# 512-column passes over both parts of the moving tile, second feed-forward matrices by columns, smaller modulation loads, in a four-layer fp32 block program on one core

## The reference

```
x = x + concat(moba, mlstm, swa)(rms_norm(x, ln1) @ w_in) @ w_out
x = x + square(relu(rms_norm(x, ln2) @ w_up)) @ w_down            # 1024 -> 4096 -> 1024, two layers

mod = silu(c) @ w_ada + b_ada                                      # 6 vectors of 1024 for each layer
h = rmsnorm(x, norm1) * (1 + scale1) + shift1 ; p = h @ w_in       # 1024 -> 5632
x = x + gate1 * ((sigmoid(a) * (retention @ w_ret_o) + sigmoid(b) * (pool @ w_pool_o)) @ w_out)
h = rmsnorm(x, norm2) * (1 + scale2) + shift2
x = x + gate2 * ((silu(h @ w_gate) * (h @ w_value)) @ w_ffn_out)   # 1024 -> 2 x 2816 -> 1024, two layers
out = rmsnorm(x, final_norm)
```

## Time and profile before

| | |
|---|---|
| runs shown | 1609.57 us median of 3 (1604.56 to 1612.28) |
| profiled execution | 1605.11 us, of it the span 1603.3 us |
| granted TensorE clock, mean | 0.966 |
| TensorE passes (PE) | 1510.1 us, 11756 |
| weight loads (PEld) | 1444.4 us, 11756 |
| VectorE (DVE), ScalarE (ACT) | 1162.3 us, 790.5 us |
| DMA | 292.45 MB, mean 182 GB/s |
| first MLP; second | 202.9 to about 392; 575 to about 764 |
| feed-forwards of the second block | 985 to about 1178; 1403 to 1592 |

### The profile page before, as it was taken

The page is one execution under the profiler, slowest core; times in us unless marked ns, Lnnn a source line. Parts: engine busy times, 40 slices in busy tenths (PEclk is TensorE's granted clock), DMA queues, the critical chain, the costliest instruction groups (busy, mean ns, idle before and its releaser), DMA issues. The chain is left out here.

```text
span 1603.3 us, 28167 instructions
## 1 busy us (share of the span) xinstructions
PE 1510.1 (94%) x11756; PEld 1444.4 (90%) x11756; DVE 1162.3 (72%) x1907; ACT 790.5 (49%) x1208; POOL 10.5 (1%) x21
## 2 busy tenths in 40 slices
PE   5887999999987989999999999999999999999998
PEld 5875789999875679999999899999999999999997
DVE  4777768886778768877666787888876678775554
ACT  3544554444534554444646564444455666354443
POOL 2000000000000000000000000000000000000000
PEclk7997999999998899999999999999999999999999
DMA  8331278994532158986655556888666445556652
GB/s 242 103 107 64 68 225 287 303 287 138 153 106 92 51 191 275 300 278 208 172 157 149 154 158 211 268 289 272 224 173 180 146 145 157 157 174 185 187 186 75
DMA packets 382431, 292.45 MB, mean 182 GB/s; under 512 B 12749, under 2 KB 340689, under 8 KB 382049
## 3 DMA queue, kind: packets, MB, share of 16 engines
q1 hardware_dynamic: 380928, 287.01, 58.6%
q10 hardware_dynamic: 672, 1.97, 0.4%
q0 software_dynamic: 704, 1.66, 0.3%
HBM read 289.56 MB, written 1.05 MB: 181 GB/s over the span
## 5 line engine op out<-in xcount | busy, mean ns | idle before, releaser
L732 DVE TENSOR_TENSOR w_lo<-raw,w_hi 128x1024 fp32r<-128x1024 f32 x450 | 548.5, 1220 | 147.9 <-ACT w_hi L451 146.2
L451 ACT ACTIVATE w_hi<-raw 128x1024 fp32r<-128x1024 f32 x450 | 465.0, 1047 | 64.4 <-DMA raw<-in_w_out 29.6
L1331 PE MATMUL mx<-h_hi,w_hi 128*128 128x258 f32 (+1 forms) x1216 | 347.1, 285 | 8.0 <-DVE h_lo L753 7.3
L1331 PE MATMUL acc<-h_hi,w_hi 128*128 128x258 f32 (+1 forms) x1136 | 342.1, 301 | 10.5 <-DVE w_lo L732 5.3
L1333 PE MATMUL mx<-h_hi,w_lo 128*128 128x258 f32 (+1 forms) x1216 | 343.9, 283 | 0.0
L1332 PE MATMUL mx<-h_lo,w_hi 128*128 128x258 f32 (+1 forms) x1216 | 343.8, 283 | 0.0
L1333 PE MATMUL acc<-h_hi,w_lo 128*128 128x258 f32 (+1 forms) x1136 | 325.9, 287 | 0.0
L1332 PE MATMUL acc<-h_lo,w_hi 128*128 128x258 f32 (+1 forms) x1136 | 325.6, 287 | 0.0
L1339 PE MATMUL acc<-u_hi,w_hi 128*128 128x256 f32 x864 | 244.4, 283 | 1.4 <-DVE u_lo L1078 1.4
L1340 PE MATMUL acc<-u_lo,w_hi 128*128 128x256 f32 x864 | 242.1, 280 | 0.0
L1341 PE MATMUL acc<-u_hi,w_lo 128*128 128x256 f32 x864 | 242.0, 280 | 0.0
(11 more groups left out here) (257 smaller groups left out, 1854.3 us busy)
## 6 DMA issues: line engine op xcount, KB each, us to landing
raw<-in_w_in SPq DMA_DIRECT2D x132, 512.0 KB, 3.8
ada<-in_w_ada SPq DMA_DIRECT2D x48, 1024.0 KB, 6.6
raw<-in_w_ffn_in SPq DMA_DIRECT2D x88, 512.0 KB, 3.9
raw<-in_w_up SPq DMA_DIRECT2D x64, 512.0 KB, 6.5
raw<-in_w_down SPq DMA_DIRECT2D x64, 512.0 KB, 5.3
raw<-in_w_ffn_out SPq DMA_DIRECT2D x44, 512.0 KB, 3.4
raw<-in_w_out SPq DMA_DIRECT2D x32, 512.0 KB, 3.7
raw<-in_w_ret_o SPq DMA_DIRECT2D x16, 512.0 KB, 3.9
```

Source lines behind the costliest of these rows:

```text
L451: nc.scalar.activation(w_hi[:, n % NS], raw[:, n % NS], ACT.Copy).then_inc(hi_ready, 1)
L732: V.tensor_tensor(w_lo[:, n % NS], raw[:, n % NS], w_hi[:, n % NS].bitcast(F32), ALU.subtract).then_inc(lo_ready, 1)
L1331: mm(outp, wh, rhs_hi(k), start=k == 0, stop=False)
```

## The change

1. `h_hi`/`h_lo`, `y_hi`/`y_lo` and `u_hi`/`u_lo` become halves of one tensor with both parts of a tile side by side (`h2`, `y2`, `u2`). In the MLPs, the retention output, the second block's output and its feed-forward's output matrix, a tile takes one pass of `w_hi` over both parts (512 columns, a whole bank) and one pass of `w_lo` over the high part into the bank's second half (`both`, `slab_both`). Whoever reads the bank now adds its two halves: ScalarE copies one, VectorE adds the other, or VectorE adds both to x in turn. The projections, the pool slabs, `w_ffn_in` and the first block's output keep three passes.
2. `w_down` and `w_ffn_out` go by columns: first all 32 (44) slabs of the first matrix, with all of u kept on chip, then 32 (22) slabs, four (2.75) for each 128 output features, in three banks of `mx` in turn. A `w_ffn_out` slab that spans two chunks is loaded in two pieces. `row_slab`, `row_tail` and the orders `MLP` and `FFN` go. rstd is applied after the second matrix, squared (`rstd2`), in the MLP. Residual, norm and the next stage's operand follow tile by tile (`norm_hi_tile`, `low_tile`, `square_tile`) behind each chunk; the last transposes too.
3. Modulation weights come in 96 loads of 512 KB, spread over six stages: 48 products in each MLP, 16 in the first 16 projection slabs of each second-block layer, 48 and 16 in the feed-forwards. A group's sum stands on TensorE one position, its columns on VectorE two positions after its eighth product. TensorE waits for `ada_out` before `partners2(0)`.
4. In the pool slabs the rounding of `y_hi` moves from VectorE to ScalarE, behind it the low part, with a conversion between.

The core of the diff (other edits follow from these):

```diff
+ADA_UNITS = 4
+ADA_PLAN = {
+    ("A", 0): (0, 6, lambda q: 4 + q * 28 // 20 if q < 20 else 32 + q - 20),
+    ("A", 1): (6, 6, lambda q: 4 + q * 28 // 20 if q < 20 else 32 + q - 20),
+    ("P", 0): (12, 2, lambda q: 4 + q * 10 // 16),
+    ("F", 0): (14, 6, lambda q: 5 + q * 38 // 34 if q < 34 else 44 + (q - 34) * 18 // 14),
+    ("P", 1): (20, 2, lambda q: 4 + q * 10 // 16),
+    ("F", 1): (22, 2, lambda q: 6 + 2 * q),
+}
+def ada_loads(stage):
+    g0, n, at = ADA_PLAN[stage]
+    return [(NS + i if i < 3 else at(2 * i - 5) + 1 + NS, g0 * ADA_UNITS + i) for i in range(n * ADA_UNITS)]
+def ada_sums_at(stage, later):
+    g0, n, at = ADA_PLAN[stage]
+    return {at(8 * i + 7) + later: g0 + i for i in range(n)}
...
+                for d in range(32):
+                    n, s = divmod(d, 4)
+                    i = a_mlp[l] + MLP_UP + d
+                    load(i, raw[:, i % NS], wdown_v[:, l * 32 + 8 * s:l * 32 + 8 * s + 8, n * P:(n + 1) * P])
+                    ada_upto(pending, MLP_UP + d)
...
+                for j in range(MLP_UP // 2):
...
+                    hi_upto(at + AHEAD)
+                    act.wait_ge(slab_used, at + 2)
+                    nc.scalar.activation(sqt[:, 0], acc[:, b:b + 2, S:], ACT.Copy).then_inc(u_small, 1)
                     hi_upto(at + AHEAD + 1)
+                    act.wait_ge(u_pos, l * 16 + j + 1)
+                    nc.scalar.activation(t, t, ACT.Relu).then_inc(u_relu, 1)
+                    hi_upto(at + AHEAD + 2)
...
+                    lo_upto(at + AHEAD)
+                    dve.wait_ge(u_small, l * 16 + j + 1)
...
+                    V.tensor_tensor(ru[:, j % 2].rearrange("p (c t) -> p c t", c=2), acc[:, b:b + 2, 0:S], sqt[:, 0],
+                                    ALU.add).then_inc(u_pos, 1)
                     lo_upto(at + AHEAD + 1)
+                    if j:
+                        low(j - 1)
+                    ada_beside(2 * j)
+                    ada_beside(2 * j + 1)
+                    lo_upto(at + AHEAD + 2)
...
                     V.scalar_tensor_tensor(up[:, 0:S], up[:, 0:S], up[:, S:S + 1], gate[:, 0:S], ALU.add, ALU.mult).then_inc(g_prod, 1)
-                    while l == 0 and q < 64 and ada_step_b(q) == u:
-                        ada_product(128 + q)
-                        q += 1
-                    lo_upto(at + AHEAD + 2)
+                    ada_beside(2 * u)
+                    ada_beside(2 * u + 1)
+                    if u < 21:
+                        lo_upto(at + AHEAD + 2)
...
+            def both(bank, i, j, part, first, last):
+                mm(halves(bank), w_hi[:, i % NS, j], part, start=first, stop=False)
+                return mm(bank[:, S:], w_lo[:, i % NS, j], part[:, 0], start=False, stop=last)
...
+                sums = ada_sums_at(("P", l), 1)
+                for i in range(16):
+                    project(i)
+                    if i in sums:
+                        ada_sums(sums[i])
                 pe.wait_ge(bp_sh, e0 + 8)
+                pe.wait_ge(ada_out, (14, 22)[l])
                 partners2(0)
...
+                for s in range(FFN_IN):
...
+                    slab(f0 + s, h2, acc[:, s % 4, 0:W],
...
+                    ada_after(s)
```

More of the change, by code:

```diff
@@ L365, in load_ada @@
             def load_ada(e):
-                g, half = e // 2, e % 2
+                g, part = divmod(e, ADA_UNITS)
                 if e >= 3:
@@ L763, in boundary @@
                         norm_squares(v, b - 1)
[L764 removed]
+                    if b < 3:
                         norm_low(v, b, gain)
[L766 removed]
                 norm_squares(v, 3)
             def norm_squares(v, b):
[L770 removed]
+                dve.wait_ge(n_sq, N_SQ[v] + b + 1)
                 if b:
                     if b > 1:
[L773 removed]
+                        dve.wait_ge(n_acc, N_ACC[v] + b - 1)
                     V.tensor_tensor(ssq[:], ssq[:], sqt[:, b % 2], ALU.add).then_inc(n_acc, 1)
@@ L814, in ada_columns, with beside, work @@
                                 ALU.add).then_inc(ada_out, 1)
+            def beside(stage):
+                tiles, columns = ada_tiles(stage), ada_sums_at(stage, 2)
+                def work(p):
+                    for q in tiles.get(p, ()):
+                        ada_product(q)
+                    if p in columns:
+                        ada_columns(columns[p])
+                return work
             def norm_gain(l):
@@ L1100, in _ @@
+                low(MLP_UP // 2 - 1)
                 v = l * 2 + 2
@@ new lines, in _ @@
+                for d in range(32):
+                    n, s = divmod(d, 4)
+                    if n >= 3 and s == 0:
+                        pe.wait_ge(x_ready, 8 * (l * 2 + 2) + n - 2)
+                    slab_both(m0 + MLP_UP + d, lambda k: u2[:, 8 * s + k], mx[:, 1 + n % 3], first=s == 0, last=s == 3,
+                              before=(lambda k: pe.wait_ge(u_ready, l * 16 + 4 * s + k // 2 + 1)) if n == 0 else None,
+                              ).then_inc(slab_used, 1)
+                    ada_after(MLP_UP + d)
@@ new lines, in _ @@
+                    ada_after(s)
+                ends = 0
+                for d in range(22):
+                    i = f0 + FFN_IN + d
+                    pe.wait_ge(lo_ready, i + 1)
+                    for at, n, k0, count in ffo_runs(d):
+                        if n >= 3 and k0 == 0:
+                            pe.wait_ge(x_ready, 8 * (l * 2 + 6) + n - 2)
+                        for k in range(k0, k0 + count):
+                            if n == 0:
+                                pe.wait_ge(g_ready, l * 22 + k + 1)
+                            ins = both(mx[:, 1 + n % 3], i, at + k - k0, u2[:, k], k == 0, k == 21)
+                        if k == 21 and not FFO_WHOLE[n]:
+                            ins.then_inc(chunk_done, 1)
+                    ins.then_inc(slab_used, 1)
+                    ada_after(FFN_IN + d)
+                    if l == 1 and d >= 2 and d - 2 in FFO_END:
+                        to_tokens(FFO_END.index(d - 2))
```

589 lines of the change are left out of this document (308 added, 281 removed).

## The result

The changed kernel takes 1642.93 us (median of 4 runs, 1638.59 to 1649.5) against 1609.04 for the kernel before: a ratio of 1.0216, 95% interval 1.0174 to 1.0259. It is slower by 34 us, where I had forecast some 6 less, and it lies above my range (1579 to 1620).

A forecast was written before the change was run, and what follows sets the result against it. TensorE's number of passes times their pitch, plus its waits, was taken as the bound; gains of 46.6 us less costs of 40.7 gave net -5.9, 1605.1 to 1599.2, on the median 1604 us, range 1579 to 1620.

The forecast's parts named there:

- Passes: Converted tiles, MLPs and output stages: one 512- and one 256-column pass replace three of 256, gaining 34 us (bounds 0 and 36).
- a 512-column pass should cost 215: TensorE's converted tiles: a 512-column pass hides its weight load and takes 215 ns; a 256-column pass still 117 to 119.
- rival 2: Every converted tile: the 512-column pass gives less, 224 ns (net +8 us) to 235 (net +28); decides from 219; chance 0.16.
- Waits: TensorE waits for modulation sums in feed-forwards and MLP up phases, and before the projection's rotation: 25.4 us (bounds 12, 32).
- 2.9 us from pass to pass. 4 x 2.9 = 11.6: Feed-forward sums at even positions, two per layer: TensorE waits 2.9 us each for VectorE's work behind the pair, 11.6 together.
- 0.8 each: Feed-forward sums at odd positions (21, 39): a slab more of room but two products, 0.8 us each, 1.6 together.
- Covered, at 83 to 86%: MLP up and down phases: VectorE's and ScalarE's work fits within TensorE's slab time, 4.4 of 5.34 us and 9.2 of 10.7.
- Clock: Half-clock stretches behind TensorE's stops: new ones cost 13.2 us (bounds 3 and 20), removed ones give back 6.5.
- rival 3: Down phase short of DMA or VectorE, slabs taking the time of their loads: net +4 us, up to +10; chance 0.14.
- rival 4: Passes overlap further than any row shows, a tile at two pitches of 117 ns: 191 us less; chance 0.01.
- the gate's gain: Mixer's output gate: moving the rounding to ScalarE cuts TensorE's wait from 2.95 us to 1.9, twice, a gain of 2.2.
- the small costs: Late landings of loads, 1.5 us (bounds 0 and 8), and a conversion behind the norm at layer 1's start, 0.6.

The follow-up runs named there:

- e3: Changed kernel with ScalarE's rounding of the next slab's weights ahead of its wait for the scaled gate in the feed-forward's first phase; 1626.84 us, ratio 1.0116.
- e2: Changed kernel with TensorE's modulation sums two positions later in MLPs and feed-forwards and their columns two later; 1598.42 us, ratio 0.9941.
- e6: Changed kernel with late modulation sums, ScalarE's rounding first in the feed-forward, and the second block's projection products ending one slab sooner; 1588.41 us, ratio 0.9885.
- e9: e6 with ScalarE's second sigmoid (the pool's gate) behind its first two copies of the retention output instead of ahead of them; 1584.88 us, ratio 0.9853.

## Why the prediction was wrong

The sum was -5.9 us and it came to +38.3: 44 us missed, in three terms.

- **Passes.** I put 34 us; the three prices are 14.5, 7.3 and 10.2 by the medians (14.8, 8.0 and 8.0 by the ratios), the slabs themselves say 12, so 20 to 27 us of the 44 are here. The step that failed is "a 512-column pass should cost 215": I took the price from an fp32 pass of 512 cycles, and explained the 117 ns of the narrow pass by its weight load. Alone, the wide pass measured 227 and in the kernel 230 to 235, and no narrower load made it shorter: the pass does not hide the 10 ns. That is the near end of rival 2 ("if the 10.4 ns belong to the pass and not to the load, it costs 224"), and h and y, at 235 and 233, are at its far end. The pitch is beyond the 219 from which that rival was to decide, and its chance of 0.16 was far too low for a case where no row of the trace had the operation. The Trainium skill ("TensorE: Matmul & The Clock Gate", section "Back-to-back issue gap") gives 216 ns for an isolated pass of 512 columns; these runs show 227 for this operand, and the measurement decides. Two slips in the working change nothing: at 213 ns the bound of the term is 37 and not 36, and at 235 the net is +27 and not +28.
- **Waits.** 25.4 us forecast, 38.1 measured. The places and the sizes of the MLP's (8.1 for 8.2), the rotation's (4.2 for 4.0) and the base size of the feed-forward's (2.99 for 2.9) were right, and no stop came in the down phases. The step that failed is "2.9 us from pass to pass. 4 x 2.9 = 11.6", and with it "0.8 each": they take it that VectorE stands ready when the slab ends and that its instructions then follow each other, as in the earlier trace rows. In the changed kernel the conversion in their midst waits for ScalarE's rounding, and the four came to 20.6 us, the two of 0.8 to 4.6, with one of 0.7 besides. The check of the engines, "Covered, at 83 to 86%", is of the MLP, where the stops came as forecast; for the feed-forward's pair I made none. Adding up busy time wouldn't have shown it either: VectorE's work for a pair is 6.47 - 1.19 = 5.28 us, under TensorE's 5.72, but the chain from VectorE to ScalarE and back takes 6.47. Of the 4.99 us by which the longest stop exceeds the 2.99 of e3, 3.71 are lag and 1.28 the wait in the last pair; of layer 1's 1.35, 1.27 are that wait. Moving one rounding ahead of one wait made all four 2.99.
- **Clock.** Net 6.7 us forecast (13.2 less 6.5), 16 measured, or 12.6 by the work that fell into the stretches. That a stop draws 3.4 or 6.8 us was right for most, but the longest drew 10.2, and the feed-forwards have 34 us at half clock where they had 6.8. The MLPs' new stops, which I had priced at half odds, drew none in this execution, but the first block has 10 us more at half clock than before, which no new stop explains. In the mixers 17 us at half clock became 10.2, about the 3.1 us that I had taken off, though not where I had: the stretches at 942.7 and 1379.6 follow the new stops in the retention output and that at 1406.9 the gate's, and the stops ahead of the pool's product (2.59 us) drew none this time, which is luck (in e2, e6 and e9 they did).
- **Right, and small.** The mixer's gate waits 2.14 us (1.9 forecast), the last sum ends 2.7 us after the last pass as forecast, and rival 3 did not occur: from 370 to 392 us, in a down phase, TensorE is busy 22.00 of 22.00 us at a DMA share of 0.78, and layer 0's feed-forward ran at 0.83 with no stop in e6. Nor did rival 4: a tile takes 346 to 351 ns, not 234. **Missed besides:** the stop of 2.58 us in the retention output, which ate the gate's gain: retention, pool and output together stand at 62.5 for 62.7.

The run with the rounding first (e3) has the waits that I had forecast, and is 19 us slower than the kernel before by its ratio, where I had summed to 6 faster: of these 25 us, 22 are the price of the wide pass (12 for 34). With its waits mended the change brings 20 to 25 us (1588 and 1585), where my gains less the small costs would have been 44; the difference is again that price.

## What to carry to other kernels

When work is laid beside a loop of two engines, don't stop at each engine's busy time: walk the loop once through both queues, in program order, and compare its period with the bound engine's. A consumer placed one step behind its producer turns every tenth of lag into a stop, and the stop into a stretch at half clock; two more slabs of room were worth 44 us here. And where a change rests on an operation that the trace does not have, the row nearest in cycles is not the row nearest in kind.

## What the runs showed of the hardware

- A pass of this operand type with weights of its own, alone and quiet, has a pitch of 111 ns at 128 and at 192 columns, and from 256 on its columns at 2.4 GHz and 13 to 14 ns: 120 at 256, 147 at 320, 173 at 384, 227 at 512, with up to 7 ns more around 416 to 496 (207 at 448). Neither the weights' columns nor the banks make the wide one shorter. An fp32 pass of 256 columns has 216, 2 to 3 ns over 512 cycles.
- Two halves of the moving tile 258 columns apart cost 6 ns more than 512 in a row (233 for 227). In turn with a narrow pass, 512 in a row have 236 too, and the narrow one 117. A pair has 353 alone, 347 on u and 352 on h in the changed kernel.
- The same stop may draw a stretch at half clock or not. The 2.41 us ahead of 257.35 drew none, in the run with the rounding first the same stop drew 6.8 us; the 1.62 us behind it drew none in the one and 3.4 in the other. In the feed-forwards every stop of 2.9 us and more drew one, in all of these runs.
